# Loading and masking an attention bias earlier in GpSimd's program, among the streamed modulation weights

## The reference

```python
mod_x = (jax.nn.silu(c) @ ada_w[layer] + ada_b[layer])[:, None, :]
mod_c = jax.nn.silu(c_ctx) @ ada_w[layer] + ada_b[layer]
sh1, sc1, g1, sh2, sc2, g2 = jnp.split(mod_x, N_MOD, axis=-1)
...
hx = modulate(rmsnorm(x, norm1_g[layer]), sh1, sc1)
hc = modulate(rmsnorm(ctx, norm1_g[layer]), csh1, csc1)
zx = hx @ w_in[layer]
...
pool_x = multiscale_pool(px, pool_w[layer], pool_scale[layer])
attn_x = neighbourhood_attention(qx, kx, vx, kc, vc, na_rpb[layer])
x = x + g1 * (jnp.concatenate([pool_x, attn_x], axis=-1) @ w_out[layer])
...
x = x + g2 * peer(h2, peer_wq[layer], peer_keys[layer], peer_u[layer], peer_v[layer])
```

## Time and profile before

| | |
|---|---|
| median of three runs | 1586.25 us |
| the profiled execution, its own time | 1590.28 us |
| its span, first to last instruction | 1588.5 us |
| mean granted TensorE clock | 0.909 of full speed |
| busy share PE, PEld, DVE, ACT, POOL | 79%, 55%, 57%, 30%, 18% |
| moved by DMA | 512 MB, mean 322 GB/s |

### The profile page before, as it was taken

The page is one execution under the profiler, slowest core; times in us unless marked ns, Lnnn a source line. Parts: engine busy times, 40 slices in busy tenths (PEclk is TensorE's granted clock), DMA queues, the critical chain, the costliest instruction groups (busy, mean ns, idle before and its releaser), DMA issues. The chain is left out here.

```text
span 1588.5 us, 17647 instructions
## 1 busy us (share of the span) xinstructions
PE 1260.7 (79%) x6148; PEld 874.5 (55%) x6148; DVE 899.3 (57%) x1790; ACT 478.9 (30%) x1165; POOL 284.9 (18%) x295
## 2 busy tenths in 40 slices
PE   7998887999777766756757655877679998988996
PEld 4886555664323326656734522655459984746772
DVE  1776337768799846589978885544442534511001
ACT  3104312333323324334443732211132232612112
POOL 0120003334433342123222221211100000000000
PEclk7998898999999997987977877999989998999997
DMA  9991138999999998999998999999968665356883
GB/s 382 357 338 35 54 106 353 424 414 427 427 427 427 427 420 322 425 409 384 400 427 328 369 360 377 403 425 425 412 203 303 211 214 209 107 192 248 296 309 119
DMA packets 71987, 511.98 MB, mean 322 GB/s; under 512 B 8145, under 2 KB 8289, under 8 KB 10977
## 3 DMA queue, kind: packets, MB, share of 16 engines
q0 software_dynamic: 40400, 290.46, 44.9%
q1 hardware_dynamic: 30496, 216.78, 36.3%
q10 hardware_dynamic: 1008, 3.67, 0.7%
HBM read 509.83 MB, written 1.05 MB: 322 GB/s over the span
## 5 line engine op out<-in xcount | busy, mean ns | idle before, releaser
L935 PE MATMUL bank<-arena,diag 128*128 128x512 f32 x512 | 239.6, 618 | 55.7 <-ACT diag L1385 55.7
L960 PEld LDWEIGHTS bank<-act_t,ring 128*128 128x128 f32 x2048 | 244.4, 199 | 45.0 <-issue 38.9
L960 PE MATMUL bank<-act_t,ring 128*128 128x128 f32 x2048 | 248.7, 283 | 25.3 <-DMA ring<-in_weights 19.6
L1901 DVE SCALAR_TENSOR_TENSOR junk<-arena,bank 128x1024 f32<-128x1024 f32 x128 | 155.8, 1217 | 123.9 <-DMA arena<-in_experts,arena 123.7
L633 POOL DMA_INDIRECT arena<-in_experts,arena x128 | 130.0, 1016 | 435.5 <-DVE junk L1912 402.7
L935 PEld LDWEIGHTS bank<-arena,diag 128*128 128x128 f32 x512 | 97.0, 196 | 190.6 <-issue 111.8
L1895 DVE SCALAR_TENSOR_TENSOR junk<-arena,bank 128x1024 f32<-128x1024 f32 x128 | 153.8, 1220 | 60.2 <-DMA arena<-in_experts,arena 57.0
L609 POOL DMA_INDIRECT arena<-in_experts,arena x128 | 128.0, 1000 | 316.2 <-PE bank L935 173.9
L1912 DVE SCALAR_TENSOR_TENSOR junk<-arena,junk 128x1024 f32<-128x1024 f32 x127 | 162.7, 1281 | 4.8 <-ACT arena L1405 4.7
L970 PE MATMUL bank<-ring,act_t 128*128 128x256 f32 x576 | 131.6, 388 | 10.5 <-DMA ring<-in_weights 10.2
L1256 ACT ACTIVATE arena<-bank 128x512 f32<-128x512 f32 x74 | 43.5, 597 | 293.7 <-PE bank L970 57.5
(11 more groups left out here) (274 smaller groups left out, 1615.5 us busy)
## 6 DMA issues: line engine op xcount, KB each, us to landing
ring<-in_weights SPq DMA_DIRECT2D x203, 1024.0 KB, 6.5
arena<-in_ada_weights POOLq DMA_DIRECT2D x16, 1024.0 KB, 8.0
arena<-in_experts,arena POOLq DMA_INDIRECT x256, 13.3
row<-in_rows_in ACTq DMA_DIRECT2D x6, 512.0 KB, 3.8
arena<-in_rpb POOLq DMA_DIRECT2D x4, 512.0 KB, 14.8
res<-in_x SPq DMA_DIRECT2D x1, 1024.0 KB, 9.5
arena<-in_ctx_in SPq DMA_DIRECT2D x1, 1024.0 KB, 8.4
arena<-in_keys_in POOLq DMA_DIRECT2D x1, 1024.0 KB, 11.1
```

The lines of the kernel that those rows point to most:

```text
L935: last = mm(bank(j), diag[:, k % 4, :], bufs[k % N_BUF][:, D + half * 512:D + half * 512 + 512], start=(k == 0), stop=(k == SLOTS - 1))
L960: last = mm(b[:, at + m * P:at + m * P + P], w[:, c, m * P:m * P + P], act_t[:, c, t * P:t * P + P], start=(c == 0), stop=(c == C - 1))
L1901: v.scalar_tensor_tensor(junk[:, 0, :], bufs1[k % N_BUF1][:, 0:D], 1.0, x_nat_at(1), ALU.mult, ALU.mult, accum_out=dots[:, 1, k:k + 1]).th ...
```

## The change

Two constants give the places: the bias is loaded behind unit 3 (it was behind unit 7), and the mask's wait and the mask itself stand behind the load of unit 9 (they stood behind the load of unit 15 and of `keys`). Nothing else moves, and the same instructions run.

```diff
+BIAS_LOADED, BIAS_MASKED = 3, 9
...
                 pool.dma_start(ada_ring[a % ADA_RING], ada_weights[a]).then_inc(ada_loaded[a % ADA_RING], 16)
-                if a == 7:
+                if a == BIAS_LOADED:
                     for r in range(4):
                         lo = (r % 2) * GRID
                         pool.dma_start(bias[lo:lo + GRID, r // 2], rpb[:, :, 3 - r:7 - r, :]
                                        .rearrange("w h i c -> w h (i c)")).then_inc(bias_loaded, 16)
+                if a == BIAS_MASKED:
+                    pool.wait_ge(bias_loaded, 64)
+                    pool.wait_ge(c1_loaded, 16)
+                    flat = bias.rearrange("p t h (i c) -> p (t h i) c", c=GRID)
+                    nc.gpsimd.tensor_tensor(flat, flat, win_mask.unsqueeze(1).broadcast_to([P, 64, GRID]), ALU.add)\
+                        .then_inc(bias_masked, 1)
             pool.dma_start(keys, keys_in).then_inc(keys_loaded, 16)
-            pool.wait_ge(bias_loaded, 64)
-            pool.wait_ge(c1_loaded, 16)
-            flat = bias.rearrange("p t h (i c) -> p (t h i) c", c=GRID)
-            nc.gpsimd.tensor_tensor(flat, flat, win_mask.unsqueeze(1).broadcast_to([P, 64, GRID]), ALU.add)\
-                .then_inc(bias_masked, 1)
```

## The result

The changed kernel took 1595.98 us (median of nine runs, 1592.32 to 1601.95) against 1587.14 us before: ratio 1.0063, 95% interval 1.0043 to 1.0083. Timed again beside the kernel before in a later job it gave 1.0084 (1.0065 to 1.0103). The forecast of 1598.8 us against 1586.25 is a ratio of 1.0079. So the change makes the kernel slower, by 10 to 13 us.

The account below looks back on a forecast made before the run. TensorE was taken as the bound, VectorE's late units counting only where late for their sums. 12.3 + 2.0 + 0 - 1.8 = +12.5 us on 1586.25 gave 1598.8 us, range 1593.0 to 1603.0.

Parts of the forecast that it names:

- The bound and the place: TensorE is the bound up to 128.6 us; units 4 and 5 are ready only 0.9 us before TensorE wants them.
- Term 1: Ahead of step 4: unit 4 lands late behind the bias, TensorE starts step 4 12.3 us later (9.6 to 14.6).
- Unit 5 right behind unit 4: On VectorE: unit 5 follows unit 4 without a pause, since its load lands 2.6 us later, less than unit 4's 3.93.
- Term 2: TensorE behind its pause ahead of step 4: work at half clock costs 2.0 us (1.7 to 2.6).
- Term 3: Mask behind unit 9: it slows VectorE's unit 7 by 8.9 us, just covered at TensorE, so 0.
- Term 4: The last sum, unit 15 on TensorE: the wait of 1.76 us goes, -1.8 us.
- The sum: Whole kernel: 12.3 + 2.0 + 0 - 1.8 = +12.5 us, 1598.8 us against 1586.25.
- Nothing later takes it back: From 131 us on every stage waits for the one ahead, so the +12.5 us reaches the end.
- Rival 1: At unit 4's landing: unit 4 does not queue behind the bias and lands by 60.5; 1584.5 us, chance 0.05.
- Rival 2: Ahead of step 4: the bias costs only its bytes, 5.1 us; +4 in all, 1590.3 us, chance 0.08.
- Rival 3: At unit 7: the mask lands on the path too, 3 to 7 us late; +16 to +21, about 1605, chance 0.07.
- Signs: New profile: unit 4's load 20 to 24 us, mask start near 85, pooling matmuls near 143, same durations from there on.

Follow-up runs that it names:

- e1_load_only: Against the kernel before, only the bias load moved, to behind unit 3; the mask stayed last. Ratio 1.0089 (1.0070 to 1.0109).
- e8_again: The changed kernel with no edit, timed again beside the kernel before in a further job. Ratio 1.0084 (1.0065 to 1.0103).
- e4_long_rows: Changed kernel with the bias stored so each DMA reads 8 KB in one piece per partition, still 64 partitions. Ratio to the kernel before 1.0087.
- e5_all_partitions: Changed kernel with the four bias DMAs each writing all 128 partitions, 4 KB per partition. Ratio to the kernel before 1.0031.
- e3_mask_last: Kernel before, bias behind unit 7, with the mask last and waiting until VectorE is through with unit 15. Ratio 0.9988 (0.9969 to 1.0006).
- e7_wide_last: Kernel before, bias behind unit 7 in DMAs writing 128 partitions, mask last behind VectorE's unit 15. Ratio 0.9983 (0.9965 to 1.0002).
- e6_own_queue: Changed kernel with the four bias DMAs started from ScalarE's queue, behind its first evacuation, not GpSimd's. Ratio to the kernel before 1.0050.

## Why the prediction was right, step by step

- **The bound and the place.** Right: VectorE's lead of 0.9 us at units 4 and 5 was the whole cover. e1_load_only shows that the load's new place alone loses everything.
- **Term 1, +12.3 us.** The mechanism was right, the size too small: 85.24 - 69.15 = 16.1 us (85.09 in the second execution), above the term's own upper end of 14.6. Unit 4 started at 76.4 (76.2), not 73.0, later than my latest landing of 74.6 and than the 70 to 75 us to which I had given 0.80. From 46 to 76 us the engines moved 12 x 0.316 + 18 x 0.288 = 8.98 MB; less the bias, 6.88 MB at 409 GB/s are 16.8 us, so the bias cost 13.2 us of all engines where I had 12.0, and the rest 1.2 us more than the 15.6 I had counted (12.0 until unit 4's old landing, 3.6 of ring). That adds 2.4 of the 3.4 us.
- **The rest of term 1.** Of the other 1.0, 0.6 is that I took a value below my own sum of 73.6, and 0.4 lies between the window's end and VectorE's start. How the 2.4 divide is not firm: in e8_again (322 GB/s over the 30 us) the same sum gives 11.5 us for the bias and 2.9 too few for the rest. I had allowed "up to a microsecond more" for engines that go on with later units: of units 5 and 6, 2.1 MB, only 1.35 MB were moved behind unit 4's landing, so some 0.75 MB, 1.8 us at 409 GB/s (an estimate), had gone ahead of it. The last 0.4 of the 3.8 us missed are the sum of unit 5, which took 1.02 us at half clock. I had also noted the two rates and not asked why the bias was slow. e4_long_rows and e5_all_partitions answer it: because each DMA fills half of the partitions, not because of its pieces.
- **Unit 5 right behind unit 4.** Right: 3.93 us (76.38 to 80.31).
- **Term 2, +2.0 us for the clock.** Right in kind. Measured 1.5 us (8.66 - 7.15), below the stated 1.7 to 2.6, and 2.6 in the second execution, 2.9 and 3.1 in e1_load_only and e4_long_rows (10.01 and 10.21). The difference is when the granted clock leaves 0.50: between 88 and 89 us in the changed kernel, between 90 and 91 in e8_again and e4_long_rows. Why it does so at different times stays open. The wait of 2.50 us in e5_all_partitions was enough for 1.7 us (8.84).
- **Term 3, 0 for the mask.** Right: unit 7 is ready at 100.9, TensorE comes for it at 101.1, and no wait stands there. The margin is 0.2 us, as in the forecast (97.6 against 97.8, both 3.3 us too early). VectorE's seven operations took 12.39 us, as 12.48 before.
- **Term 4, -1.8 us.** Right, and incomplete: the wait of 1.76 us had also left TensorE at half clock behind it (0.50 granted from 131 to 134 us; 5.39 us for the first 16 pooling matmuls, 3.70 without). The step "what was lost at the last sum" should have read 3.5 us. I had listed the clock for the new pause and not for the old one. e3_mask_last and e7_wide_last show both parts gone.
- **The sum.** +16.1 + 1.5 + 0 - 1.8 = +15.8 at the pooling's start (15.67 measured), less 1.7 us behind it: 14.0. I had 12.5. Term 1 was 3.8 us too small, term 2 0.5 too large, and term 4 missed 1.7 us of gain; that these partly cancel is luck. The total is nearer than its terms.
- **"Nothing later takes it back."** Right as far as the runs can tell. The first profile had only 11.7 us left at the first gather and 5.3 in the span, but the way from the gather to the end took 1340.2 to 1349.9 us over the ten profiled executions, whatever the kernel (1340.2 is the changed kernel's own, the shortest). e8_again, with 14.2 us left at the gather, has the ratio 1.0084.
- **Rival 1** fell in its kernel; e6_own_queue shows the condition that it needs. **Rival 2** fell here, but its arithmetic (5.1 us for the bytes, unit 4 at 64.6, 4.0 us lost ahead of step 4) comes near e5_all_partitions: an estimated 4.9 us, unit 4 at 65.18, step 4 at 73.62, 4.5 us later, ratio 1.0031. **Rival 3** fell: the mask cost VectorE its own length and no more (12.39 us for seven operations that take 3.62).
- **Signs.** Unit 4's load took 26.1 us where I had 20 to 24, the mask began at 89.15 and not near 85, the pooling matmuls at 146.5 and not near 143, all by the late landing. "From there on the same durations" failed for the first pooling matmuls (3.70 and 5.39 us), for the clock missed in term 4.

## What to carry to other kernels

Before a transfer is moved earlier in a queue, look at the lead of what stands behind it, not at the idle time of the engine: in the old place 12.45 us of VectorE's idle time were free, in the new one VectorE had 0.9 us to spare, and TensorE stood for 13 us. Ask of each transfer what share of the engines' rate it gets (bytes over the time at full share); 200 to 290 GB/s at full share beside 409 to 427 meant a tile written half the partitions at a time, and one layout change took half to two thirds of the loss away. Count a wait together with the half clock behind it: here 1.8 us of waiting cost 3.5.

## What the runs showed of the hardware that I had not expected

- DMAs into 64 partitions hold all 16 engines busy for more than twice as long as their bytes ask for: by the estimate above 11.4 to 13.2 us for 2.10 MB (the changed kernel twice, e4_long_rows), against 4.9 us into 128 partitions; 243 against 423 GB/s at full share, the pieces being 8 KB and 4 KB.
- Starting a DMA can hold the engine that starts it: 14.0 us for the fourth start on ScalarE, with three slow transfers in its queue. The same DMAs cost GpSimd 2.77 us for four. No run shows what the fourth start waited for.
- The clock column can miss a slow stretch. Some executions run the front of the first projection at half speed behind a pause of 1.4 us: 6 matmuls in two microseconds instead of 11, and 15.68 us for the 64 of the changed kernel where the kernel before took 14.05. The window from 38 to 40 us, first of the kernel before, then of the changed one, then of e3_mask_last:

```profile
38.00:40.00 2.00, 2.00 (x11) 1.77 (x10) 1.29 (x3) 0.86 (x3) 0.00 (x0) 1.00 1.02 401
```

```profile
38.00:40.00 2.00, 2.00 (x6) 1.55 (x6) 1.31 (x3) 0.89 (x3) 0.00 (x0) 1.00 1.00 408
```

```profile
38.00:40.00 2.00, 2.00 (x6) 1.55 (x6) 1.25 (x3) 0.83 (x3) 0.00 (x0) 0.50 1.03 410
```

The second and the third row have the same six matmuls, once with a granted clock of 1.00 and once with 0.50; the durations decide. This moves the sums behind steps 0 and 1 from 50.9 to about 52.8 us, in four of the ten profiled executions (the changed kernel, e1_load_only, e3_mask_last, e5_all_partitions). Where TensorE later waits for VectorE, as in the changed kernel, it is absorbed; in e3_mask_last it is not.
